# State-space layer of a hybrid backbone: its input projections put through the split 1 MB stream, inputs laid out beforehand, decay matrices merged

## Chip, cores, metric

One core of a Trainium2 chip. The metric is the device time of one launch in microseconds (us), over three runs.

## What is computed

Two layers work on 512 tokens of width 1024 (256 of context, 256 latent), in float32. Layer 0 is a state-space layer (SSD, 32 heads in 8 groups, state 128, chunks of 128 tokens, forward and backward) and a dense SwiGLU of width 2816. Layer 1 is windowed attention and eight SwiGLU experts of width 3584 (two for each token). Norms are scaled and shifted by rows computed from `silu(c) @ w_mod`. What the change touches is the state-space layer:

```python
zxbcdt = h @ w_in                       # 512 x 1024 by 1024 x 6208: z 2048, x 2048, B 1024, C 1024, dt 64
xbc = silu(depthwise_conv_same(xbc, conv_w, conv_b))          # 5 taps along the tokens
dt = softplus(dt_raw + dt_bias); a = -exp(a_log) * dt; acum = cumsum(a)       # in each chunk
decay = exp(where(lower, acum[i] - acum[j], -inf))
y = (C B^T * decay * dt) x + (C state) * exp(acum)            # and the same backward
out = gated_rmsnorm(y, z, norm_w) @ w_out                     # RMS in each of the 8 groups
```

## The kernel before

**Engines and order.** Each engine has one instruction stream in an order that is written out by hand. They meet at named semaphores (`gemm_done`, `tok_evac`, `st_op`, `y_ready` ...). SP issues nearly all DMAs in one such order too, so a wait in it holds back every later load. Tokens lie along the free axis (`hT` is 8 tiles of 128 features by 512 tokens).

**Start.** 22 small vectors are loaded as rows and transposed, x and ctx are loaded by tokens and transposed (32 transposes, L642), then four 2 MB pieces of `w_mod` give shift and scale of the first norm (L618, rows turned to columns at L628), and only then come the norm, the dt projection (L662) and the first projections (L673).

**The state-space loop.** `step(g)` runs for each of the 8 groups. TensorE: projections `gemm_tile` of group g+1 (six tiles: two of x, then B and C, two of z; 8 float32 matmuls of 128x128 by 512 each, which the profile counts as 16 instructions, L673), `group_norm(g-1)` (L699), `to_tokens(g)` (transposes and C B^T, L708 to L716), `states(g)` (L724), one piece of `w_mod` (`modulation`, L618), `outputs(g)` (L745), `turn_mod` (L628). VectorE: the convolution of group g+1 (L1686, L1688), gating (L1757, L1761), `segments` (acum_i - acum_j for 4 heads and both directions, L1699), the group's 1/RMS over 128x512 (L1659, L1664), `token_scales` (L1710, x times tail, x times dt), `decayed` (L1717, L1722), `state_ops` (L1730 to L1743), `skip` (L1750). ScalarE: evacuations (L1254, L1259, L1300), exponentials of the decays (L1303, L1306), silu (L1287), squares and root (L1313, L1296). GpSimd masks the segments (L577). SP fetches the rows of acum, spread over all partitions, with `load_rowb` (L425, two DMAs of 1 MB), once `y_ready` of the group before says that `rowb` is free.

**Behind the loop.** Weights come as 1 MB units through a ring of four (`d_raw`). For each, ScalarE rounds a high part (`dense_high`, L1219), VectorE subtracts it (`dense_low`, L1552), and TensorE adds three fp32r products for one float32 product (`thrice`, L793 to L795): `w_out`, the SwiGLU, qkv and `w_o`. The experts' 336 units are treated alike in a ring of 12 (L1435, L1950, L1052 to L1054).

## Time and profile before

| | |
|---|---|
| median of 3 runs (lowest, highest) | 2409.55 us (2407.49, 2412.07) |
| profiled execution, its own time | 2407.64 us |
| its span | 2405.7 us |
| busy: TensorE, VectorE, ScalarE, GpSimd | 93%, 64%, 47%, 2% |
| start until the first projection | 0 to 70.5 us |
| state-space loop, until group 7 is alone | to 550.9 us |
| end of group 7 and `w_out` | to about 695 us |
| SwiGLU, attention, router | to about 1350 us |
| experts | to the end |

The shares of busy time are means over stages with different limits. The chain of waits says which engine's work ended last in each stage; the lines say what one instruction costs.

### The profile page before, as it was taken

The page shows a single profiled execution, that of the slowest core. Times are in us where ns is not written, and L with a number is a line of the kernel's source. Part 1 is how long each engine was busy: PE and PEld are TensorE (multiplying, and loading weights), DVE is VectorE, ACT ScalarE, POOL GpSimd, SP SyncE. Part 2 cuts the span into 40 slices and gives each one's busy share as a digit, 9 for nine tenths or more (in the row PEclk, how much of TensorE's full clock was granted, in tenths as well). Part 3 has the DMA queues.
Part 4 walks back from the last instruction along what each step waited for, and adds up shares of the span by engine and source line. Part 5 has one row for each costly group of instructions (what it writes and reads, how often), then busy time and mean ns, then how long its engine had stood idle before and what let it go on. Part 6 is the DMA issues. An engine that isn't in the chain of part 4 may idle for free.

```text
span 2405.7 us, 27018 instructions
## 1 busy us (share of the span) xinstructions
PE 2238.5 (93%) x10771; PEld 1662.0 (69%) x10771; DVE 1539.7 (64%) x1554; ACT 1137.0 (47%) x1084; POOL 56.4 (2%) x21
## 2 busy tenths in 40 slices
PE   4999999996889999998898799999999999999997
PEld 3355555554767777786756688787878888887875
DVE  1387766666432333223585688887878788887885
ACT  1333333334232222224353676667666667676763
POOL 0030001111000000000000000000000000000000
PEclk8999999998989999998899899999999999999998
DMA  8243333321225545533600599999999989999990
GB/s 275 63 151 113 122 122 122 122 73 67 88 70 175 164 154 172 167 100 75 191 22 33 217 369 347 336 342 334 346 336 346 358 325 364 335 346 336 344 337 36
DMA packets 258467, 504.86 MB, mean 210 GB/s; under 512 B 34434, under 2 KB 148724, under 8 KB 256308
## 3 DMA queue, kind: packets, MB, share of 16 engines
q1 hardware_dynamic: 258276, 503.19, 59.8%
q8 instruction: 76, 1.25, 0.2%
q14 instruction: 35, 0.29, 0.0%
q10 hardware_dynamic: 80, 0.13, 0.0%
HBM read 502.08 MB, written 1.18 MB: 209 GB/s over the span
## 4 chain that ended last, share of the span: by engine, by line
PE 86%; DVE 3%; ACT 2%; issue 1%; DMA 0%; DVEq 0%; SPq 0%; ACTq 0%
PE ps L1054 13%; PE ps L1052 13%; PE ps L1053 13%; PE ps L673 11%; PE ps L793 8%; PE ps L795 7%; PE ps L794 7%; PE ps L745 3%; PE ps L963 1%; PE ps L981 1%; PE ps L1038 1%; PE ps L1111 1%; PE ps L1081 1%; PE ps L805 1%; PE ps L971 1%
## 5 line engine op out<-in xcount | busy, mean ns | idle before, releaser
L1950 DVE TENSOR_TENSOR w_lo<-w_raw,w_hi 128x2048 fp32r<-128x2048 f32 x336 | 749.4, 2286 | 52.1 <-ACT w_hi L1435 51.0
L1435 ACT ACTIVATE w_hi<-w_raw 128x2048 fp32r<-128x2048 f32 x336 | 626.6, 1920 | 79.5 <-PE ps L1054 79.0
L1052 PE MATMUL ps<-w_hi,x_hi 128*128 128x512 f32 x896 | 358.0, 400 | 2.0 <-DVE x_lo L2006 2.0
L1054 PE MATMUL ps<-w_hi,x_lo 128*128 128x512 f32 x896 | 355.5, 397 | 0.0
L1053 PE MATMUL ps<-w_lo,x_hi 128*128 128x512 f32 x896 | 352.3, 393 | 0.0
L673 PE MATMUL ps<-hT,ring 128*128 128x512 f32 x768 | 335.1, 594 | 2.5 <-ACT area L1279 2.5
L1552 DVE TENSOR_TENSOR d_lo<-d_raw,d_hi 128x2048 fp32r<-128x2048 f32 (+1 forms) x52 | 117.0, 2251 | 328.8 <-ACT d_hi L1219 328.8
L1219 ACT ACTIVATE d_hi<-d_raw 128x2048 fp32r<-128x2048 f32 (+1 forms) x52 | 97.8, 1881 | 374.3 <-DMA d_raw<-in_ffn_w 224.8
L673 PEld LDWEIGHTS ps<-hT,ring 128*128 128x128 f32 x768 | 144.1, 190 | 177.0 <-issue 174.2
L1054 PEld LDWEIGHTS ps<-w_hi,x_lo 128*128 128x128 f32 x896 | 168.2, 188 | 41.3
L1053 PEld LDWEIGHTS ps<-w_lo,x_hi 128*128 128x128 f32 x896 | 168.3, 188 | 40.1
L1052 PEld LDWEIGHTS ps<-w_hi,x_hi 128*128 128x128 f32 x896 | 168.3, 188 | 40.1 <-DVE x_lo L2006 2.2
L1052 PE MATMUL ps<-w_hi,h_hi 128*128 128x512 f32 x448 | 180.4, 403 | 1.4 <-DVE h_lo L2022 1.4
L793 PE MATMUL ps<-h_top,d_hi 128*128 128x512 f32 (+1 forms) x432 | 170.0, 394 | 9.9 <-DVE h_low L1544 9.9
L1054 PE MATMUL ps<-w_hi,h_lo 128*128 128x512 f32 x448 | 177.7, 397 | 0.0
L1053 PE MATMUL ps<-w_lo,h_hi 128*128 128x512 f32 x448 | 176.2, 393 | 0.0
L795 PE MATMUL ps<-h_top,d_lo 128*128 128x512 f32 (+1 forms) x432 | 166.0, 384 | 0.0
L794 PE MATMUL ps<-h_low,d_hi 128*128 128x512 f32 (+1 forms) x432 | 164.6, 381 | 0.0
L793 PEld LDWEIGHTS ps<-h_top,d_hi 128*128 128x128 f32 x432 | 82.8, 192 | 35.4 <-issue 18.0
L1054 PEld LDWEIGHTS ps<-w_hi,h_lo 128*128 128x128 f32 x448 | 84.1, 188 | 20.7
L1052 PEld LDWEIGHTS ps<-w_hi,h_hi 128*128 128x128 f32 x448 | 84.1, 188 | 20.6 <-DVE h_lo L2022 1.6
L1659 DVE RECIPROCAL area<-area 128x512 f32<-128x512 f32 x8 | 26.8, 3353 | 111.5 <-ACT area L1296 96.9
(275 smaller groups left out, 2969.0 us busy)
## 6 DMA issues: line engine op xcount, KB each, us to landing
w_raw<-in_moe_w SPq DMA_DIRECT2D x672, 512.0 KB, 4.5
d_raw<-in_ffn_w SPq DMA_DIRECT2D x60, 512.0 KB, 4.6
ring<-in_w_mod SPq DMA_DIRECT2D x48, 512.0 KB, 5.8
d_raw<-in_w_mod SPq DMA_DIRECT2D x48, 512.0 KB, 6.4
ring<-in_ssd_w_in SPq DMA_DIRECT2D x32, 512.0 KB, 5.1
area<-acum_rows SPq DMA_DIRECT2D x16, 1024.0 KB, 5.9
ring<-in_ssd_w_in SPq DMA_DIRECT2D x8, 1024.0 KB, 5.4
d_raw<-in_ssd_w_out SPq DMA_DIRECT2D x16, 512.0 KB, 4.9
```

The lines of the kernel that those rows point to most:

```text
L673: last = mm(ps[t % 2][:], wtile(slot, 8, 768, k, t * P), hT[:, k, :], start=k == 0, stop=k == KT - 1)
L745: last = mm(o, l, r, start=n == 0, stop=n == len(steps) - 1)
L793: mm(o, w[0], v[0], start=first, stop=False)
L794: mm(o, w[0], v[1], start=False, stop=False)
L795: return mm(o, w[1], v[0], start=False, stop=last)
L1052: mm(o, hi, w_hi[u % HIGH][:, a:a + 512], start=first, stop=False)
L1053: mm(o, hi, w_lo[u % RAW][:, a:a + 512], start=False, stop=False)
L1054: return mm(o, lo, w_hi[u % HIGH][:, a:a + 512], start=False, stop=last)
L1219: A(d_hi[si % D_HIGH][:, 0:w], d_raw[n % D_RAW][:, 0:w], ACT.Copy).then_inc(S["dhi_done"], 1)
L1435: A(w_hi[n % HIGH][:], w_raw[n % RAW][:], ACT.Copy).then_inc(S["whi_done"], 1)
L1552: TT(d_lo[n % D_RAW][:, 0:w], d_raw[n % D_RAW][:, 0:w], d_hi[si % D_HIGH][:, 0:w].bitcast(F32), ALU.subtract).then_inc(S["dlo_done"], 1)
L1950: TT(w_lo[n % RAW][:], w_raw[n % RAW][:], w_hi[n % HIGH][:].bitcast(F32), ALU.subtract)\
```

## The change

- `w_in` and layer 0's `w_mod` join the ring of 1 MB units. Each projection of a group is now three units ("x", "bc", "z") of 48 fp32r products, split by `dense_high` and `dense_low` as the later weights are. The norm's output is split too (`h_top`, `h_low_`), and so is the dt weight (`wdt`).
- All inputs are packed outside the kernel: x is stored transposed, the vectors as one 128x536 array, each unit of weights as 128 rows of 8 KB. The row loads, their transposes and those of x are gone. The experts' stream reads packed units as well.
- The first norm's shift and scale come in four pairs of units (`mod_pair`, `turn_pair`). After each pair two feature tiles of the norm are finished, and `gemm_part` takes these two of the first x projection.
- The mask is applied to `rowb` itself. `segments` is now on ScalarE: exp(acum_i + nb_j) with nb = ln(dt) - acum as bias, 32 ACTIVATEs of 128x128 in a group. Both directions are added (`merge`) and multiplied by C B^T once, and x times dt is gone. The outputs have 80 instead of 112 instructions. Only the 768 columns that carry a state are exponentiated and multiplied in `rowb` (`row_exps`, `carried`).
- The convolution's middle tap with its bias is on ScalarE (`tap`); the other four stay on VectorE, x and B/C apart.
- The group's RMS is summed into 128x128 and spread by TensorE (`group_sums`, `group_spread`).
- The gated rows of groups 2 to 5 are written to DRAM (`keep_group`) and read back into `hT`. The loops over groups are unrolled.

```diff
-    order = [("wout", j, h) for j, h in ((0, 0), (1, 0), (0, 1), (1, 1), (2, 0), (2, 1), (3, 0), (3, 1))]
+    order = [("m0", u, 0) for p in range(4) for u in (p, 4 + p)]
+    order += [("x", 0, 0), ("bc", 0, 0), ("z", 0, 0)]
+    for g in range(GROUPS):
+        if g + 1 < GROUPS:
+            order += [("x", g + 1, 0), ("bc", g + 1, 0)]
+        else:
+            order.append(("wout", 0, 0))
+        order += [("m0", 8 + 2 * g, 0), ("m0", 9 + 2 * g, 0)]
+        if g + 1 < GROUPS:
+            order.append(("z", g + 1, 0))
+    order += [("wout", j, h) for j, h in ((1, 0), (0, 1), (1, 1), (2, 0), (2, 1), (3, 0), (3, 1))]
...
+            def load_dense(n):
+                if D_BEFORE[n] is not None:
+                    sp.wait_ge(S["d_used"], D_BEFORE[n] + 1)
+                w = dense_width(DENSE[n]) // 2
+                for i in range(2):
+                    sp.dma_start(d_raw[D_SLOT[n]][:, i * w:i * w + w], dense[n, :, i * w:i * w + w])\
+                        .then_inc(d_in[D_SLOT[n]], 16)
...
             def load_rowb(g):
+                if g == 0:
+                    sp.wait_ge(S["scr_out"], 16)
+                else:
+                    sp.wait_ge(S["y_ready"], 2 * g)
...
+                    src = scr[d * HEADS + g * HPG:d * HEADS + g * HPG + HPG, :]
                     sp.dma_start(rowb[d], src.unsqueeze(0).to_broadcast([P, HPG, NTOK])).then_inc(S["rowb_in"], 16)
-            sp.dma_start(cst[:, 0:C_BAND], consts[:, 0:C_BAND]).then_inc(S["consts_in"], 16)
-            sp.dma_start(cst[:, C_IOTA:C_N], consts[:, C_IOTA:C_N]).then_inc(S["band_in"], 16)
-            sp.wait_ge(S["zero_done"], 1)
...
             for n, unit in enumerate(DENSE):
+                if n < 4 or unit == EARLY:
+                    continue
+                if unit[0] == "m0" and 8 <= unit[1] < 23 and unit[1] % 2:
+                    load_rowb((unit[1] - 9) // 2)
...
+            for g in range(GROUPS):
+                pl.wait_ge(S["rowb_in"], 32 * g + 32)
+                if g:
+                    pl.wait_ge(S["y_ready"], 2 * g)
                 for d in range(2):
-                    pl.wait_ge(S["seg_op"], 2 * g + d + 1)
-                    v = seg[d].rearrange("p h (c i) -> p (h c) i", c=NCH)
-                    pl.affine_select(out=v, in_=v, compare_op=ALU.is_ge, fill=-1e30, base=0,
+                    pl.affine_select(out=seg[d].rearrange("p h (c i) -> p (h c) i", c=NCH),
+                                     in_=rowb[d].rearrange("p h (c i) -> p (h c) i", c=NCH),
+                                     compare_op=ALU.is_ge, fill=-1e30, base=0,
                                      pattern=[[0, 16], [1 if d == 0 else -1, P]],
                                      channel_multiplier=-1 if d == 0 else 1).then_inc(S["seg_mask"], 1)
...
+            def gemm_part(kind, g, banks, ks):
+                n = D_AT[(kind, g, 0)]
+                dense_wait(n)
+                for k in ks:
+                    if g == 0:
+                        pe.wait_ge(S["n_low"], k + 1)
+                    for t in range(2):
+                        last = thrice(ps[banks[t]][:], dense_tile(n, k, t), (h_top[:, k, :], h_low_[:, k, :]),
+                                      k == 0, k == KT - 1)
+                return last
+            def group_sums(g):
+                pe.wait_ge(S["ysq_done"], 2 * g + 2)
+                pe.wait_ge(S["mod_done"], 5 + g)
                 for t in range(2):
-                    last = mm(ps[5][:], ones, ysq[:, t, :], start=t == 0, stop=t == 1)
+                    for c in range(NCH):
+                        last = mm(ps[4][32 * c:32 * c + 32, 0:P], ones[:, 0:32], ysq[:, t, c * P:c * P + P],
+                                  start=t == 0, stop=t == 1)
                 last.then_inc(S["gsum_done"], 1)
...
+                for c in range(NCH):
+                    pick = ident[:, 32 * c:32 * c + 1].to_broadcast([P, P])
+                    last = mm(ps[5][:, c * P:c * P + P], pick, grs, start=True, stop=True)
...
-                            steps = [(xdt[d][:, ch, c0:c0 + HD], seg[d][:, h, s]) for d in range(2)]
+                            steps = [(xtok[:, ch, c0:c0 + HD], seg[0][:, h, s])]
...
-            def step(i, first=False, more=True):
-                if more:
-                    gemm_tile(i + 1, 0, 0).then_inc(S["gemm_done"], 1)
-                    gemm_tile(i + 1, 0, 1).then_inc(S["gemm_done"], 1)
-                if not first:
...
-                if more:
-                    gemm_tile(i + 1, 0, 2).then_inc(S["gemm_done"], 1)
-                    gemm_tile(i + 1, 0, 3).then_inc(S["gemm_done"], 1)
-                states(i)
...
-                if more:
-                    gemm_tile(i + 1, 0, 4).then_inc(S["gemm_done"], 1)
-                    gemm_tile(i + 1, 0, 5).then_inc(S["gemm_done"], 1)
...
-            with pe.Fori(1, 7) as i:
-                step(i)
...
+            norm_sum(0)
+            for p in range(4):
+                mod_pair(p, 5 + p % 2)
+                turn_pair(p, 3 + p % 2)
+                if p == 0:
+                    norm_spread(0)
+                else:
+                    gemm_part("x", 0, (0, 1), (2 * p - 2, 2 * p - 1))
...
+            pe.wait_ge(S["mrow_sb"], 4)
+            for k in range(KT):
+                c = slice(P * k, P * k + P)
+                last = thrice(ps[6][:], (wdt_hi[:, c], wdt_lo[:, c]), (h_top[:, k, :], h_low_[:, k, :]), k == 0, k == KT - 1)
+            last.then_inc(S["dt_ps"], 1)
+            pe.wait_ge(S["gemm_evac"], 2)
+            gemm_part("bc", 0, (0, 1), range(KT)).then_inc(S["d_used"], 1)
+            pe.wait_ge(S["dt_dve"], 1)
...
+            pe.wait_ge(S["mod_done"], 4)
+            gemm_part("z", 0, (2, 3), range(4))
...
+            gemm_part("z", 0, (2, 3), range(4, KT)).then_inc(S["d_used"], 1)
...
+            for g in range(7):
+                if g:
+                    group_sums(g - 1)
+                pe.wait_ge(S["gemm_evac"], 6 * g + 4)
+                gemm_part("x", g + 1, (0, 1), range(4))
+                if g:
+                    group_spread(g - 1)
+                gemm_part("x", g + 1, (0, 1), range(4, KT)).then_inc(S["d_used"], 1)
+                to_tokens(g)
+                pe.wait_ge(S["gemm_evac"], 6 * g + 8)
+                gemm_part("bc", g + 1, (0, 1), range(4))
+                states(g)
+                gemm_part("bc", g + 1, (0, 1), range(4, KT)).then_inc(S["d_used"], 1)
+                pe.wait_ge(S["tok_evac"], 4 * g + 4)
+                mod_pair(4 + g, 5)
+                if g == 0:
+                    pe.wait_ge(S["ac_rows_sb"], 1)
+                outputs(g)
+                gemm_part("z", g + 1, (2, 3), range(KT)).then_inc(S["d_used"], 1)
+                turn_pair(4 + g, 4)
...
+            def tap(g, t):
+                act.wait_ge(S["gemm_evac"], 6 * g + t + 1)
+                if g:
+                    act.wait_ge(S["sk_done" if t < 2 else "ce_done"], 2 * g if t < 2 else 3 * g)
+                    act.wait_ge(S["tr_ready"], 4 * g)
+                A(cx[:, t, :].rearrange("p (s t) -> p s t", s=2), raw[:, t, :, 2:2 + 256], ACT.Identity,
+                  bias=vc(V_CB + conv_row(g, t)), scale=vc(V_CW + 64 + conv_row(g, t))).then_inc(S["tap_done"], 1)
...
+                if not g:
+                    act.wait_ge(S["nb_op"], 2)
+                for d in range(2):
+                    act.wait_ge(S["seg_mask"], 2 * g + d + 1)
+                    for h in range(HPG):
+                        for ch in range(NCH):
+                            v = seg[d][:, h, ch * P:ch * P + P]
+                            j = 32 * d + 4 * g + h
+                            last = A(v, v, ACT.Exp, bias=nb[:, ch, j:j + 1])
+                    last.then_inc(S["e_done"], 1)
...
+                act.wait_ge(S["e_done"], 2 * g + 2)
+                for d, c in CARRIED:
+                    v = rowb[d][:, :, c]
+                    A(v, v, ACT.Exp).then_inc(S["er_done"], 1)
...
+            for p in range(4):
+                one_tile(2 * p)
+                one_tile(2 * p + 1)
+                top_tile(0, 2 * p)
+                top_tile(0, 2 * p + 1)
+                if p == 0:
+                    dense_high(0)
+                if p == 1:
+                    act.wait_ge(S["wdt_in"], 16)
...
+                evac_z(g, 0)
+                evac_z(g, 1)
+                conv_silu(g, 2)
+                conv_silu(g, 3)
+                if g:
+                    group_root(g - 1)
+                dense_high(3 * g + 4)
+                segments(g)
+                evac_raw(g + 1, 0)
+                evac_raw(g + 1, 1)
+                token_evac(g)
+                row_exps(g)
+                dense_high(3 * g + 5)
+                tap(g + 1, 0)
+                tap(g + 1, 1)
+                evac_raw(g + 1, 2)
+                evac_raw(g + 1, 3)
+                if g < 6:
+                    dense_high(3 * g + 6)
+                tap(g + 1, 2)
+                tap(g + 1, 3)
+                conv_silu(g + 1, 0)
+                conv_silu(g + 1, 1)
+                y_squares(g)
...
+            def convolve(g, bc):
+                base = 16 * g + 8 * bc
+                for i, k in enumerate((0, 1, 3, 4)):
+                    for q in range(2):
+                        t = 2 * bc + q
+                        if i == 0:
+                            dv.wait_ge(S["tap_done"], 4 * g + t + 1)
+                        else:
+                            dv.wait_ge(S["conv_step"], base + 2 * (i - 1) + q + 1)
+                        dst = cx[:, t, :].rearrange("p (s t) -> p s t", s=2)
+                        STT(dst, raw[:, t, :, k:k + 256], vc(V_CW + 32 * k + conv_row(g, t)), dst, ALU.mult, ALU.add)\
+                            .then_inc(S["conv_step"], 1)
...
-            def segments(g):
-                dv.wait_ge(S["rowb_in"], 32 * g + 32)
+                return v[:, :, 32 * d + 4 * g:32 * d + 4 * g + 4]
+            def token_scales(g):
...
+            def merge(g):
+                dv.wait_ge(S["e_done"], 2 * g + 2)
+                TT(seg[0], seg[0], seg[1], ALU.add).then_inc(S["m_add"], 1)
+            def carried(g):
+                for i, (d, c) in enumerate(CARRIED):
+                    dv.wait_ge(S["er_done"], 3 * g + i + 1)
+                    v = rowb[d][:, :, c]
+                    TT(v, v, cx[:, 3, c].unsqueeze(1).to_broadcast([P, HPG, v.shape[2]]), ALU.mult)\
+                        .then_inc(S["ce_done"], 1)
...
+            for g in range(7):
+                if g:
+                    mod_out(3 + g)
+                    group_inverse(g - 1)
+                dense_low(3 * g + 4)
+                if g:
+                    finish(g - 1)
                 token_scales(g)
+                merge(g)
+                carried(g)
                 decayed(g)
                 state_ops(g)
                 skip(g)
-                convolve(g + 1)
-                mod_rows(4 + g, (5,), 512)
+                mod_rows(4 + g)
+                dense_low(3 * g + 5)
+                convolve(g + 1, 0)
                 gated(g)
-            dv.wait_ge(S["dcol_op"], 3)
-            convolve(0, first=True)
-            step(0, first=True)
-            with dv.Fori(1, 7) as g:
...
```

## Rows read from the trace of the kernel before

**Rows 1.** Windows: length, busy by engine, clock share, DMA share, GB/s.

```profile
40.00:60.00 20.00, 16.50 (x128) 10.49 (x128) 3.18 (x8) 0.37 (x1) 0.00 (x0) 0.59 1.07 328
...
1400.00:1500.00 100.00, 100.00 (x460) 81.63 (x459) 83.68 (x52) 69.59 (x49) 0.00 (x0) 1.00 0.97 355
```

**Rows 2.** Chain that ended last: start, length, what; outputs of groups 0, 3, 4, 6, 7, `w_out`'s end.

```profile
155.66 7.13 PE ps L745 x112
...
342.85 7.13 PE ps L745 x112
...
404.64 7.13 PE ps L745 x112
...
528.21 8.73 PE ps L745 x112
...
606.85 7.10 PE ps L745 x112
...
694.01 1.67 DVE xT L1809 x4
```

**Rows 3.** Waits of TensorE, 100 to 600 us: in total, times, longest.

```profile
PE ps L745 <- DVE ring L1743: 19.5, 7, 3.5
PE ps L699 <- DVE modT L1591: 15.5, 1, 15.5
```

**Rows 4.** The same chain in the SwiGLU: 48 fp32r matmuls lie between the rows.

```profile
722.03 1.00 PE ps L805 x16
734.33 0.34 PE ps L816 x4
734.67 1.00 PE ps L805 x16
```

**Rows 5.** Lines, 0 to 700 us: busy us, mean ns, idle before.

```profile
L1688 DVE SCALAR_TENSOR_TENSOR area<-area,col 128x512 f32<-128x512 f32 x128 | 85.5, 745 | 0.0
...
L1722 DVE TENSOR_TENSOR area<-area,ring 128x2048 f32<-128x2048 f32 x16 | 35.9, 2284 | 3.9 <-ACT area L1306 3.9
...
L1552 DVE TENSOR_TENSOR d_lo<-d_raw,d_hi 128x2048 fp32r<-128x2048 f32 x10 | 22.9, 2290 | 35.4 <-ACT d_hi L1219 35.4
...
L1219 ACT ACTIVATE d_hi<-d_raw 128x2048 fp32r<-128x2048 f32 x10 | 19.1, 1909 | 38.3 <-PE ps L795 27.7 <-PE ps L618 6.4 <-DMA d_raw<-in_ssd_w_out 4.2
...
L724 PE MATMUL ps<-area 128*128 128x256 f32 x96 | 22.0, 379 | 0.0
```

**Rows 6.** TensorE in order of time: start, length.

```profile
30.39 3.64 PE L618 MATMUL ps<-ring,csT 128*32 128x512 f32 x32 [1.31 <-issue]
...
70.47 14.00 PE L673 MATMUL ps<-hT,ring 128*128 128x512 f32 x32
85.19 0.71 PE L684 MATMUL ps<-cst,area 64*128 64x64 f32 x8 [0.72 <-DVE area L1644]
...
114.28 0.60 PE L694 MATMUL ps<-cst,acum 128*64 128x128 f32 x4
```

**Rows 7.** GpSimd's masks (source view): ns, least, median, most.

```profile
L577 POOL TENSOR_SCALAR_AFFINE_SELECT area<-area x16: 1997/2163/12979, 132.2 to 568.8; 128x2048 f32<-128x2048 f32 x16
```

**Rows 8.** ScalarE's short operations in order of time: start, length together.

```profile
30.70 4.26 ACT L1171 ACTIVATE area<-xT 128x512 f32<-128x512 f32 x8 [16.20 <-DMA rw<-in_moe_router]
...
60.61 7.97 ACT L1189 ACTIVATE hT<-hT,modT,alpha 128x256 f32<-128x256 f32 x16 [3.94 <-DVE hT L1534]
...
100.75 0.45 ACT L1271 ACTIVATE acum<-ps 128x128 f32<-128x128 f32 x2 [0.28 <-PE ps L690]
101.21 1.28 ACT L1273 ACT_TABLE_LOAD   x1
```

**Rows 9.** Waits, 1340 us to the end: TensorE's longest in the experts.

```profile
PE ps L1081 <- DVE xT L2028: 6.1, 7, 0.9
```

**Rows 10.** DMA issues: number, KB each, median us to landing.

```profile
w_raw<-in_moe_w SPq DMA_DIRECT2D x672, 512.0 KB, 4.5
...
area<-acum_rows SPq DMA_DIRECT2D x16, 1024.0 KB, 5.9
```

More of the change, by code:

```diff
@@ L105, with dense_places, dense_width @@
 D_HIGH = 2
-def dense_arrivals():
-    total, out = [0] * D_RAW, []
-    for n, x in enumerate(DENSE):
-        total[n % D_RAW] += 64 if x[0] in ("q", "wo") else 32
-        out.append(total[n % D_RAW])
-    return out
-D_ARRIVED = dense_arrivals()
-W2_K = ((0, 8), (8, 8), (16, 6))
+W0 = 3 * GROUPS
+W2_K = ((0, 8), (8, 8), (16, 6))
+EARLY = ("x", 0, 0)
+MOD_PAIRS = [(p, 4 + p) for p in range(4)] + [(2 * p, 2 * p + 1) for p in range(4, 12)]
+def dense_places():
+    slot, before, arrived = [], [], []
+    last, total, ring = [None] * (D_RAW + 1), [0] * (D_RAW + 1), 0
+    for n, unit in enumerate(DENSE):
+        u = D_RAW
+        if unit != EARLY:
+            u = ring % D_RAW
+            ring += 1
+        total[u] += 32
+        slot.append(u)
+        before.append(last[u])
+        arrived.append(total[u])
+        last[u] = n
+    return slot, before, arrived
+D_SLOT, D_BEFORE, D_ARRIVED = dense_places()
+def dense_width(unit):
+    return 256 * (W2_K[unit[2]][1] if unit[0] == "w2" else KT)
 STREAM = expert_stream()
@@ new lines, in _ @@
+            last = mm(ps[4][:, 256:512], ones, atk, start=True, stop=True)
+            last.then_inc(S["ac_ps"], 1)
+            gemm_part("z", 0, (2, 3), range(4, KT)).then_inc(S["d_used"], 1)
+            pe.wait_ge(S["ac_sb"], 1)
+            for ch in range(NCH):
+                last = pe.transpose(ps[6][0:64, ch * P:ch * P + P], acum[:, ch, :], ident)
+            last.then_inc(S["ac_rows"], 1)
+            for g in range(7):
[13 more added lines that the diff above has]
+                mod_pair(4 + g, 5)
+                if g == 0:
+                    pe.wait_ge(S["ac_rows_sb"], 1)
+                outputs(g)
+                gemm_part("z", g + 1, (2, 3), range(KT)).then_inc(S["d_used"], 1)
+                turn_pair(4 + g, 4)
@@ L1322, in _ @@
+            evac_z(7, 0)
+            evac_z(7, 1)
+            conv_silu(7, 2)
+            conv_silu(7, 3)
+            group_root(6)
+            dense_high(W0)
             gate_high(0)
-            dense_high(0)
+            segments(7)
+            token_evac(7)
             gate_high(1)
-            act.wait_ge(S["gsum_done"], 7)
-            A(grs, ps[5][:], ACT.Sqrt, bias=eps, scale=1.0 / 256).then_inc(S["grs_done"], 1)
-            for n in range(4):
-                act.wait_ge(S["tr_ready"], 28 + n + 1)
-                dst = (xtok[:, 0:2, :], xtok[:, 2:4, :], btok, cbT)[n]
-                A(dst, ps[2 + n][:], ACT.Copy).then_inc(S["tok_evac"], 1)
@@ L1342, in _ @@
-            for t in range(2):
-                act.wait_ge(S["yg_done"], 14 + t + 1)
-                A(ysq[:, t, :], yb[:, t, :], ACT.Square).then_inc(S["ysq_done"], 1)
-            dense_high(3)
-            act.wait_ge(S["gsum_done"], 8)
-            A(grs, ps[5][:], ACT.Sqrt, bias=eps, scale=1.0 / 256).then_inc(S["grs_done"], 1)
+            dense_high(W0 + 2)
+            y_squares(7)
+            dense_high(W0 + 3)
+            group_root(7)
             gate_high(4)
             gate_high(5)
-            dense_high(4)
@@ L1761, in gated @@
                     TT(yb[:, t, :], yb[:, t, :], zs[:, t, :], ALU.mult).then_inc(S["yg_done"], 1)
-            def step(g, first=False):
-                segments(g)
-                if not first:
-                    mod_out(0, 12 + 4 * g, 4, 3 + g, 5)
-                    finish(g)
+            dense_low(2)
+            dv.wait_ge(S["dcol_op"], 3)
+            convolve(0, 0)
+            dv.wait_ge(S["ac_ps"], 1)
+            TS(nb, dtk, 1e-37, None, ALU.max).then_inc(S["nb_op"], 1)
+            convolve(0, 1)
+            dv.wait_ge(S["nb_ln"], 1)
+            dv.wait_ge(S["ac_sb"], 1)
+            TT(nb, nb, acum, ALU.subtract).then_inc(S["nb_op"], 1)
+            dv.wait_ge(S["ac_exp"], 1)
+            TT(tail, ps[4][:, 256:512].rearrange("p (c h) -> p c h", c=NCH), acum, ALU.subtract).then_inc(S["ac_tail"], 1)
+            dense_low(3)
+            dv.wait_ge(S["ac_exp"], 2)
+            TT(tail, tail, dtk, ALU.mult).then_inc(S["ac_tail"], 1)
+            dv.wait_ge(S["ac_tail"], 2)
+            for g in range(7):
+                if g:
+                    mod_out(3 + g)
+                    group_inverse(g - 1)
+                dense_low(3 * g + 4)
+                if g:
+                    finish(g - 1)
                 token_scales(g)
+                merge(g)
+                carried(g)
                 decayed(g)
```

1020 lines of the change are left out of this document (458 added, 562 removed).

## The prediction

> **What bounds the kernel now.** I read the page first: its shares of busy time (the table above) put TensorE far ahead. A mean over stages does not price a change in one of them, so the windows came next. Between 1400 and 1500 us TensorE is busy all the time at the full granted clock while DMA moves 355 GB/s [rows 1], and TensorE's longest wait in the experts is 6.1 us in seven pieces, none of it on a load [rows 9]. There the packed layout is worth nothing unless it slows the stream. The change lives in the first 700 us, and there I read the chain that ended last: outputs of group 0 end at 162.79 us, of group 6 at 536.94, of group 7 at 613.95, and `w_out` ends at about 694.0 [rows 2]. In the loop one group takes 404.64 - 342.85 = 61.79 us; the six periods take 374.15, or 62.4 each. Only then the waits: of a group's 61.8 us TensorE waits only 19.5/7 = 2.8 us for the state operations [rows 3]. So the loop is TensorE's own work, and the reader should see that only less work, or the same work faster, moves it.
>
> **TensorE's work in a group.** 96 instructions of float32 projection take 3 x 14.0 = 42 us, because 32 take 14.00 [rows 6]. After it 48 fp32r matmuls stand for 32 such instructions. In the SwiGLU 48 of them, 4 short ones (0.34 us) and 16 for a piece of `w_mod` (1.00 us) fill 734.67 - 722.03 = 12.64 us [rows 4]: (12.64 - 1.34)/48 = 0.235 us each, 11.2 us a unit, 33.7 us a group. Bounds: 0.217, the mean of all 460 in the window of the experts [rows 1], and 0.43 at half clock. That is 8.3 us less. The outputs lose 32 of 112 instructions, which take 7.13 us [rows 2]: 5.1, so 2.0 less. The rest stays within 0.5 us (root sums 0.5 and spread 1.0 for 1.9; two 1 us units of `w_mod` for 1.9). From 61.8 less the wait of 2.8, TensorE's work falls by 10.8 to about 48 us.
>
> **The other two engines.** VectorE gains three `dense_low` (3 x 2.29, [rows 5]) and one addition of 128x2048 (2.24, as L1722's 35.9/16). It loses the segments (eight two-input operations of 128x512; priced like L1688's 85.5/128 = 0.67 they are 5.3), x times dt (two of 128x1024, 2.2), one of two 2048-wide products by C B^T (2.24), a quarter of the two by C (1.1) and four first taps, and the reciprocal becomes a quarter as wide. 9.1 come and at least 10.8 go: no more work than now. ScalarE gains three `dense_high` (3 x 1.91), four taps (0.7 each) and the 32 exponentials of 128x128. No row shows these with a bias. Two copies of 128x128 take 0.45 together, so 0.22 each; eight of 128x512 take 4.26, 0.53 each; sixteen of 128x256 with bias and scale per partition take 7.97, 0.50 each, where the line through the first two would give 0.33 [rows 8]. One operand per partition is then worth half of 0.17: 0.31 each, 9.9 us a group. Bounds 0.22 and 0.50. It loses two exponentials of 128x2048 and a quarter of two more, some 5 us, so it gains 13 to 14. Neither engine comes to TensorE's 48, so what decides is who waits for whom.
>
> **One period by hand.** Time 0 is the end of outputs(g). TensorE: z to 11.2, `turn_pair` to 12.0. VectorE, which began `skip` when the outputs began at -5.1, does `mod_rows`, `dense_low` of z and the x taps (8 x 0.67) until 4.0, gating to 6.5, `dense_low` of x to 8.8, the B/C taps to 14.1. `mod_out` stands behind them, and `group_sums` waits for it: a new wait of TensorE, 12.0 to 14.4, with all projections queued behind. Half of x to 20.4, spread to 21.4, other half to 26.9, `to_tokens` to 29.2. ScalarE: silus to 15.4, table load 1.28 [rows 8], root 17.1, `dense_high` 19.0, table load 20.3, exponentials to 30.2, evacuation of x to 31.3. TensorE's first half of B/C needs those banks: second new wait, 29.2 to 31.4. Then 36.9, states (22.0/8 = 2.75 [rows 5]) 39.6, second half 45.1, `w_mod` 47.1. ScalarE's token copies end at 33.4, row exponentials at 36.2. VectorE: scales 34.8, merge 37.0, `carried` (3072 columns, 3.4) 40.4, product 42.6, state operations 46.8 (4.2; they end 4.8 after the states now, the wait of 2.8 and a `w_mod` piece of 2). Outputs 47.1 to 52.2. VectorE and TensorE arrive together. Some five handovers between engines lie on this path; 0.1 us for each rounds it to 52.5 us. Six periods: 6 x (62.4 - 52.5) = **59 us**.
>
> SP waits for `y_ready` before `load_rowb`, with the next `w_mod` unit and z queued behind it. Neither is needed for 20 us, and 7 MB in 52 us is 140 GB/s against 355 reached [rows 1]: hidden. The rows take some 8 us from the end of the outputs (5.9 to landing [rows 10], issue and waits). Spill and reload of the gated rows go by queue and lie beside this. With four slots each unit is requested at least two units ahead; without that cover a unit costs its 4.5 to 6 us each time.
>
> **The mask.** Of the 16 masks the shortest takes 2.00 us, the median 2.16, one 12.98 [rows 7]. That one began in group 0 when VectorE worked without a gap on pairs of inputs in SBUF, and it ended 2 us after VectorE stopped. So it has to find VectorE idle. By my schedule the rows land at 8, VectorE is idle from 14.3 until the root's reciprocal at 17.1, and two masks end by 18.5, before the exponentials want them at 20.3. That is a margin of 1.8 us. The Trainium skill (SBUF — State Buffer, Who interferes with whom) says that VectorE operations with two SBUF inputs and GpSimd operations that read SBUF exclude each other for a whole instruction, whichever starts first. By that rule, the trace agrees (12.98 against 2.16), and a mask that slips between two taps would hold the taps up by 2 us as well.
>
> **Start and group 0.** Before, the first projection starts at 70.47. After, 4.5 MB precede the first pair of `w_mod` units (15.5 us at 328 to 355 GB/s with some 2 us to begin). A pair takes 3.64 at the clock there (32 instructions [rows 6]), then copy, turn, `mod_out`, alpha, two tiles on ScalarE, their tops and lows. TensorE alternates pair and quarter of x; I get x finished at 64 instead of 84.5, with quarters at half clock (12 x 0.43), dt at 70, B/C at 81. The dt chain on VectorE and ScalarE is unchanged (85.19 - 70.47 = 14.7 us, from the dt matmuls' end to the transposes that wait for it), so z waits until 86.5 and ends at 98.6; acum is turned at 99.2 instead of 114.3 to 114.9. From there the rows must go to DRAM and come back (an estimate of 14 us: copies and issues, 5 out, 5.9 back [rows 10]), two masks, then the exponentials with nothing beside them: x of group 1 is evacuated only at 126, and TensorE waits some 15 us. Outputs end at 148.8 instead of 162.8: **14 us**. Bounds: 25, if the quarters run at full clock and loads come as asked; 0, if pair, copy, turn and tile follow one another with 2 us more in each of four rounds and the dt chain stretches.
>
> **Group 7 and w_out.** Before, TensorE waits 15.5 us in front of `group_norm` (first unit of `w_out` asked only then, segments behind it on VectorE) [rows 3]. After, the unit is there, but `gate_high(1)` stands behind segments and token copies on ScalarE, so the second half of `out_part(0, 0)` waits some 10 us. By the same bookkeeping outputs(7) ends 71.3 after outputs(6) instead of 77.0: **5.7 us**. Then 694.0 - 613.95 = 80 us become 73, since the splits for `out_part(0, 1)` are done during outputs(7) and the root is short: **7 us**. Behind that nothing changes.
>
> **Sum.** 59 + 14 + 5.7 + 7 = 85.7 us off the profiled execution's own 2407.64 (span 2405.7, 1.94 around it): 2321.9. The median of the runs shown is 1.9 above that execution: **2324**.
>
> **Rivals.**
> - *The mask misses its gap* (0.17). The next idle time of VectorE comes after `finish` at 22.8; the exponentials start at 24.9, 4.6 later, and all behind them. Seven times 4.6 is 32: 2356. For: the margin of 1.8 us. Against: the segments no longer fill VectorE.
> - *The short exponentials cost far more* (0.13). At 0.41, midway to the bound, 32 x 0.10 = 3.2 us in each of seven groups: 2346; at the bound of 0.50, 2367.
> - *TensorE closes its two waits* (0.13), because the B/C taps end early and the exponentials cost 0.22: 48.5 us a group, 24 less: 2300.
> - *The first projection is not begun earlier in effect* (0.03): group 0 ends as now, 2338.
> - *Slower than before: the packed experts' stream* (0.03). A unit's 4 KB pieces are now 8 KB apart, where the `w2` units were one run. 672 loads of 512 KB are 352 MB [rows 10]; 1024 us at 344 GB/s. At the 328 GB/s of the first weights [rows 1] they take 1074: 2374. Below 317 GB/s they take over 86 us more, and the change loses. Against: no wait for a load there now. The Trainium skill (DMA: Bandwidth & Descriptors, Latency and other measured facts) warns of row pitches at large powers of two, measured from 512 KiB on. No run here shows one.
> - The forecast itself: 0.51, own range 2309 to 2341.
>
> **Numbers.** The cases above from 2300 to 2356 hold over 0.9; unknown prices and a start between 0 and 25 us widen each by 10. I give 2292 to 2362. Within 0.2% (4.8 us) is what the measurement cannot tell from no change. Faster 0.95, same 0.02, slower 0.03.
>
> **What would show it.** Outputs of neighbouring groups 52 to 53 us apart; two waits of TensorE in each period, on `modT` and on the evacuation of x, 2 us each; masks of 2 us that end before the exponentials; the short exponentials near 0.31 us each; group 0's outputs ending near 149; the experts' stage as long as now. A period over 57 us, masks over 5 us, or a wait on a unit's load would make the prediction wrong.

## The result, and the profile after

The changed kernel takes 2299.35 us (median of 4 runs, 2299.00 to 2299.93). The kernel before took 2410.81 beside it (2407.49 to 2412.93). The ratio is 0.9539, interval 0.9523 to 0.9556: 4.6% faster. The forecast was 2324 with a range of 2292 to 2362; the gain is 25 us larger than forecast. The profiled execution took 2299.07 us (span 2297.3). Against its span the gain is 22.7 us larger (108.4 against 85.7, table below); the other 2 us were added in the forecast for the median of the runs.

The outputs are again the marks. In order of time on TensorE (start, length), groups 0, 2, 6 and 7:

```profile
134.61 4.86 PE L766 MATMUL ps<-area 128*64 128x128 f32 x80
...
235.16 4.86 PE L766 MATMUL ps<-area 128*64 128x128 f32 x80
...
436.87 4.86 PE L766 MATMUL ps<-area 128*64 128x128 f32 x80
...
510.05 4.86 PE L766 MATMUL ps<-area 128*64 128x128 f32 x80
```

Their ends against those of [rows 2]:

| stage | before, us | after, us | gain | forecast |
|---|---|---|---|---|
| start and group 0 | 162.79 | 139.47 | 23.3 | 14 |
| six periods | 374.15 (62.4 each) | 302.26 (50.4 each) | 71.9 | 59 |
| group 7 | 77.0 | 73.2 | 3.8 | 5.7 |
| `w_out`, to 588.28 | 80.0 | 73.4 | 6.7 | 7 |
| the rest | 1711.7 | 1709.0 | 2.7 | 0 |
| sum | 2405.7 | 2297.3 | 108.4 | 85.7 |

The waits of TensorE from 100 to 600 us (total, times, longest) answer to [rows 3]:

```profile
PE ps L704 <- DVE modT L1655: 9.2, 7, 1.5
PE ps L647 <- ACT area L1248: 8.3, 3, 7.0
PE ps L647 <- DVE g_lo L1621: 7.6, 2, 5.2
...
PE ps L631 <- DVE cst L1644: 3.6, 1, 3.6
PE ps L713 <- DVE area L1748: 3.1, 1, 3.1
```

The first line is the new wait on `mod_out` (1.47 us in every period; a short one follows in group 7). The second, on the evacuation of x, is 7.0 us once, in group 0, and 0.7 or less in the loop, where 2.2 were forecast each time. One period in order of time on TensorE (189.43 to 240.02; the projections lie between the rows):

```profile
200.60 0.95 PE L631 MATMUL ps<-cst 128*128 128x2 f32 x8
203.02 0.65 PE L704 MATMUL ps<-area,cst 128*32 128x128 f32 x16 [1.47 <-DVE modT L1655]
...
210.82 1.05 PE L713 MATMUL ps<-area,cst 128*128 128x128 f32 x8
...
225.06 2.75 PE L744 MATMUL ps<-area 128*128 128x256 f32 x12
...
233.30 1.93 PE L622 MATMUL ps<-d_raw,csT 128*32 128x256 f32 x32
```

The 24 products behind this wait, half of the projection of x, take 7.38 us between 203.60 and 210.98; the same 24 take 5.84 in the period from 290.64, from 304.81 on. The windows (length, busy by engine, clock share, DMA share, GB/s) say why:

```profile
204.00:211.00 7.00, 7.00 (x26) 5.58 (x25) 3.25 (x2) 6.96 (x14) 2.63 (x2) 0.76 0.17 68
305.00:311.00 6.00, 6.00 (x29) 4.93 (x29) 3.25 (x2) 5.96 (x10) 2.84 (x2) 1.00 0.24 93
```

So four of the six periods are 50.5 to 50.6 us long (a wait of 1.47 and 1.5 us lost to the clock behind it) and two are 49.96 (the same wait, full clock, then 0.65 on the evacuation). TensorE's own work is 50.59 - 1.47 - 1.54 = 47.6; 48 was forecast. ScalarE in the same period, in order of time:

```profile
204.78 0.37 ACT L1275 ACTIVATE area<-ps,small 128x128 f32<-128x128 f32 x1
...
208.26 9.48 ACT L1287 ACTIVATE area<-area,atk 128x128 f32<-128x128 f32 x32
217.65 1.05 ACT L1248 ACTIVATE area<-ps 128x512 f32<-128x512 f32 x2
```

The exponentials begin 18.8 us into the period (forecast 20.3) and take 0.296 each (0.31). GpSimd's masks and VectorE's B/C taps there, and the masks of all groups in the source view (ns: least, median, most), to be read beside [rows 7]:

```profile
200.29 6.34 POOL L587 TENSOR_SCALAR_AFFINE_SELECT area<-area 128x2048 f32<-128x2048 f32 x2 [43.62 <-DMA area<-acum_rows]
```

```profile
197.42 5.38 DVE L1742 SCALAR_TENSOR_TENSOR area<-area,col 128x512 f32<-128x512 f32 x8
```

```profile
L587 POOL TENSOR_SCALAR_AFFINE_SELECT area<-area x16: 2001/2008/4768, 102.3 to 454.9; 128x2048 f32<-128x2048 f32 x16
```

The rows arrive while the taps still run (to 202.72): the masks begin 10.9 us into the period, where the rows were forecast to land at 8. The first mask ends 2 us after the taps, the pair at 206.63, before the exponentials.

### The profile page after: what moved, and what is told of

It is laid out like the page before. It is cut to its first block, busy times and chain, and to the rows that moved or that the text cites. A ratio compares the mean times of both kernels' runs of the same rounds, so it can differ in the third digit from the quotient of the medians.

```text
span 2297.3 us, 27395 instructions
## 1 busy us (share of the span) xinstructions
PE 2161.5 (94%) x11224; PEld 1729.8 (75%) x11224; DVE 1495.1 (65%) x1479; ACT 1236.9 (54%) x1394; POOL 45.7 (2%) x20
## 3 DMA queue, kind: packets, MB, share of 16 engines
q8 instruction: 90, 1.47, 0.3%
## 4 chain that ended last, share of the span: by engine, by line
PE 83%; DVE 7%; ACT 4%; issue 1%; DVEq 0%; ACTq 0%
PE ps L1048 14%; PE ps L1046 14%; PE ps L1047 13%; PE ps L647 10%; PE ps L649 10%; PE ps L648 10%; DVE area L1742 3%; DVE d_lo L1613 2%; PE ps L957 1%; PE ps L975 1%; PE ps L1032 1%; PE ps L1105 1%; ACT area L1287 1%; PE ps L1075 1%; PE ps L659 1%
## 5 line engine op out<-in xcount | busy, mean ns | idle before, releaser
L1613 DVE TENSOR_TENSOR d_lo<-d_raw,d_hi 128x2048 fp32r<-128x2048 f32 (+1 forms) x76 | 171.9, 2262 | 334.4 <-ACT d_hi L1219 334.4
L647 PE MATMUL ps<-h_top,d_hi 128*128 128x512 f32 (+1 forms) x816 | 331.5, 406 | 25.2 <-DVE h_low L1605 9.8
L1219 ACT ACTIVATE d_hi<-d_raw 128x2048 fp32r<-128x2048 f32 (+1 forms) x76 | 143.7, 1890 | 382.8 <-DMA d_raw<-in_dense 245.2
L649 PE MATMUL ps<-h_top,d_lo 128*128 128x512 f32 (+1 forms) x816 | 322.9, 396 | 0.0
L648 PE MATMUL ps<-h_low,d_hi 128*128 128x512 f32 (+1 forms) x816 | 319.1, 391 | 0.0
L647 PEld LDWEIGHTS ps<-h_top,d_hi 128*128 128x128 f32 x816 | 158.3, 194 | 69.6 <-issue 26.2
L649 PEld LDWEIGHTS ps<-h_top,d_lo 128*128 128x128 f32 x816 | 158.1, 194 | 35.7
L648 PEld LDWEIGHTS ps<-h_low,d_hi 128*128 128x128 f32 x816 | 158.9, 195 | 33.6
L1047 PEld LDWEIGHTS ps<-w_lo,h_hi 128*128 128x128 f32 x448 | 84.2, 188 | 19.9
```

Source lines behind the costliest of these rows:

```text
L647: mm(o, w[0], v[0], start=first, stop=False)
L648: mm(o, w[0], v[1], start=False, stop=False)
L649: return mm(o, w[1], v[0], start=False, stop=last)
L1047: mm(o, hi, w_lo[u % RAW][:, a:a + 512], start=False, stop=False)
L1219: A(d_hi[si % D_HIGH][:, 0:w], d_raw[u][:, 0:w], ACT.Copy).then_inc(S["dhi_done"], 1)
L1613: TT(d_lo[u][:, 0:w], d_raw[u][:, 0:w], d_hi[si % D_HIGH][:, 0:w].bitcast(F32), ALU.subtract)\
```

## The experiments

A period below is the distance between the ends of neighbouring outputs. Kernels that ran on one chip are compared with each other; the others by their ratio to the kernel before and by their rows.

**1. Float32 on the high parts.** In `gemm_part` of the changed kernel:

```
-  last = thrice(ps[banks[t]][:], dense_tile(n, k, t), (h_top[:, k, :], h_low_[:, k, :]), ...)
+  last = mm(ps[banks[t]][:], dense_tile(n, k, t)[0].bitcast(F32), h_top[:, k, :].bitcast(F32), ...)
```

> The 48 triples of fp32r products of a group's projections become 48 float32 matmuls on the high parts alone (the low parts are still made, and left out of the sum). Sixteen float32 matmuls of this shape took 14.00 us in the kernel before, 0.875 each; a triple takes 3 x 0.235 = 0.70. Theory A (TensorE's own work sets the period): 48 x 0.17 = 8.3 us more per group, period 50.6 to about 58.5, whole kernel +50 to +60 us (2350 to 2360). Rival B (the gain came from the shorter waits and the work taken off the sides, and TensorE has room): under +15 us.

2338.23 us, ratio 0.9692 (0.9673 to 0.9712): 39 us more, short of the 50. The period is 55.7, the 16 matmuls of z take 14.00 us where the 48 products take 11.42, and what remains of the wait is 0.35:

```profile
312.20 14.00 PE L694 MATMUL ps<-h_top,d_hi 128*128 128x512 f32 x32
326.04 0.95 PE L631 MATMUL ps<-cst 128*128 128x2 f32 x8
327.33 0.64 PE L704 MATMUL ps<-area,cst 128*32 128x128 f32 x16 [0.35 <-DVE modT L1655]
```

A period's projections take 42.2 us instead of 34.8, 7.4 more, but the period grows by 5.3: the slower TensorE loses no clock and hardly waits. TensorE's work bounds this kernel, and the faster products gave away 2 of their 7.4 us.

**2. One product of three.**

```
-  last = thrice(ps[banks[t]][:], dense_tile(n, k, t), (h_top[:, k, :], h_low_[:, k, :]), ...)
+  last = mm(ps[banks[t]][:], dense_tile(n, k, t)[0], h_top[:, k, :], ...)
```

> Only the product of the two high parts is left in a group's projections; the two products with a low part are left out. TensorE's work falls by 96 x 0.235 = 22.6 us a group. Theory A (TensorE and the chain exponentials, evacuation, scales, merge, carried, product, state operations, outputs are nearly tied; VectorE was 1.5 us ahead at the outputs): the period falls by a few us only, to 45 to 48, whole kernel -15 to -40 us. Rival B (TensorE alone sets the period, the others have ample room): the period falls to about 30, whole kernel near -150 us.

2297.77 us, ratio 0.9524 (0.9503 to 0.9544): no gain at all, less than either theory expected. TensorE's waits from 139 to 440 us:

```profile
PE ps L704 <- DVE modT L1655: 58.5, 6, 11.5
PE ps L694 <- ACT area L1248: 35.3, 6, 6.5
PE ps L766 <- DVE area L1811: 26.8, 6, 5.0
```

20 us a period are handed back as waits. The periods are 48.5 and 48.7 (two of the six) or 52.8 to 54.3 (four). In the long ones the masks begin 0.4 to 1.2 us after the first tap and hold the others up (GpSimd, then VectorE):

```profile
194.31 4.58 POOL L587 TENSOR_SCALAR_AFFINE_SELECT area<-area 128x2048 f32<-128x2048 f32 x2 [47.90 <-DMA area<-acum_rows]
```

```profile
193.87 8.87 DVE L1742 SCALAR_TENSOR_TENSOR area<-area,col 128x512 f32<-128x512 f32 x8
```

The eight taps take 8.87 us instead of 5.38. The outputs run at a lower granted clock here (6.2 to 7.6 us long), so their ends blur the periods. The x taps of neighbouring groups on VectorE give the length of the other chain, the one over VectorE and ScalarE:

```profile
290.25 5.38 DVE L1742 SCALAR_TENSOR_TENSOR area<-area,col 128x512 f32<-128x512 f32 x8
...
339.91 5.38 DVE L1742 SCALAR_TENSOR_TENSOR area<-area,col 128x512 f32<-128x512 f32 x8
```

It is 49.66 us long where no mask stops the taps, and 53.15 where one does (237.10 to 290.25). That is 2 us more than TensorE's own 47.6 and 0.7 less than the changed kernel's mean period of 50.4: the two chains are nearly tied. The unchanged total hides two things: the six periods together grew by 9.6 us (to 311.9), by the stopped taps, and groups 0 and 7 became 5.6 and 4.6 us shorter (133.9 and 68.6).

**3. Wide exponentials.**

```
-  for h in range(HPG):
-      for ch in range(NCH): ... last = A(v, v, ACT.Exp, bias=nb[:, ch, j:j + 1])
+  last = A(seg[d], seg[d], ACT.Exp)
```

> The 32 exponentials of 128x128 with a bias become two of 128x2048 without one (leaves out -acum_j and the factor dt in the decays). ScalarE: 9.5 us become about 3.7 in each group. Theory A (in the loop TensorE's work binds and the exponentials have a margin of about 1.5 us): next to nothing in the six periods (0 to -1 us each), the gain in group 0 and group 7, where TensorE waits for the evacuation (7.0 us) and for g_lo (5.2 us): -8 to -14 us in all. Rival B (the short exponentials are on the path in every group): 8 x 5.8 = -46 us.

2282.77 us, ratio 0.9464 (0.9446 to 0.9483), 16.6 less, a little over theory A. Group 0 ends 7.2 us earlier (132.31) and group 7 takes 65.6 instead of 73.2. The six periods together take 300.45 instead of 302.26. The price of a short exponential, which had a rival of its own, counts in two groups of eight (14.8 of the 16.6 us).

**4. The first projection behind all pairs.**

```
-  else:
-      gemm_part("x", 0, (0, 1), (2 * p - 2, 2 * p - 1))
-  gemm_part("x", 0, (0, 1), (6, 7)).then_inc(...)
+  gemm_part("x", 0, (0, 1), range(KT)).then_inc(...)
```

> The first projection of x is issued whole after the four w_mod pairs, in place of one quarter behind each pair. Theory A (the quarters fill TensorE's waits between pairs): x ends later, by the three quarters of 3.1 to 5.3 us that no longer lie in the waits, less what full clock gives back: +4 to +9 us. Rival B (pairs wait for their loads and quarters only delay the next pair's chain): 0 or a gain of up to 3 us.

2300.22 us (2297.89 to 2303.28), ratio 0.9533 (0.9513 to 0.9554): by time no difference that these runs resolve. By the trace, that of the slowest of the four runs, outputs(0) end at 143.97 instead of 139.47 and the span is 2301.5. So the quarters between the pairs are worth about 4.5 of the 23.3 us by these two traces. Experiments 5, 6 and 7 leave the start as it was and end outputs(0) at 139.71, 140.95 and 141.65, so the 4.5 is uncertain by some 2 us.

**5. Masks twice.** In GpSimd's loop, a first `affine_select` with the same operands counts on a semaphore that the second waits for.

> Each mask is made twice, the second time over the first's output place, and the exponentials wait for the second. In the changed kernel a pair of masks ran from 200.29 to 206.6 us and the exponentials started at 208.26. Theory A (the prediction's step: a margin of 1.8 us, measured 1.7, stands against the pair): the exponentials start 2.4 us or more later in each group, +2.4 to +5 us a period, +15 to +35 us in all. Rival B (the exponentials of a direction wait for the mask of that direction alone, so the first needs only half of the pair and the second has another 4.7 us): the masks end in time, 0 to +3 us in all, unless they meet VectorE's operations after 207 us and hold these up.

2299.64 us, ratio 0.9538 (0.9519 to 0.9557): nothing, rival B. The four masks of one group (GpSimd), and the exponentials (ScalarE):

```profile
200.61 4.32 POOL L587 TENSOR_SCALAR_AFFINE_SELECT area<-area 128x2048 f32<-128x2048 f32 x1 [37.55 <-DMA area<-acum_rows]
205.06 2.01 POOL L593 TENSOR_SCALAR_AFFINE_SELECT area<-area 128x2048 f32<-128x2048 f32 x1
207.02 2.00 POOL L587 TENSOR_SCALAR_AFFINE_SELECT area<-area 128x2048 f32<-128x2048 f32 x1
209.17 3.86 POOL L593 TENSOR_SCALAR_AFFINE_SELECT area<-area 128x2048 f32<-128x2048 f32 x1
```

```profile
208.52 9.49 ACT L1293 ACTIVATE area<-area,atk 128x128 f32<-128x128 f32 x32
```

The last mask ends at 213.03, just when the second half of the exponentials begins. It collides with `dense_low`, which takes 3.93 instead of 2.29 us, where VectorE had been idle before its next wait.

**6. Experts from the original layout.** `load_unit` of the kernel before, with `mw1`, `mw3` and `mw2` as inputs.

> The experts' weights are read from their original layout, as in the kernel before, in place of the packed one. TensorE never waited for a load there in either kernel, though a load took 4.5 us to land before and 5.7 after. Theory A (hidden both ways): 0, within 3 us. Rival B (the packed pieces with their pitch of 8 KB cost the stream something): 5 to 20 us less than the changed kernel.

2299.85 us, ratio 0.9536 (0.9516 to 0.9556): nothing. The page's DMA issues (KB each, median us to landing) of this kernel, then of the changed one:

```profile
w_raw<-in_moe_w SPq DMA_DIRECT2D x672, 512.0 KB, 4.6
```

```profile
w_raw<-in_experts SPq DMA_DIRECT2D x672, 512.0 KB, 5.7
...
area<-acum_rows SPq DMA_DIRECT2D x16, 1024.0 KB, 8.4
```

The packed pieces land 1.1 us later, and TensorE waits for no load in either; between 1400 and 1500 us both read 334 to 336 GB/s.

**7 and 8. Taking away the wait on `mod_out`, and unloading VectorE.** Kernel 7: `turn_pair(p)` for p from 4 on writes PSUM bank 5 in place of 4, `mod_out` reads it there, and in `group_sums`

```
-  pe.wait_ge(S["mod_done"], 5 + g)
```

Kernel 8 keeps this and adds on ScalarE, behind `dense_high(3 * g + 5)`, what VectorE loses:

```
+  A(stt_[:, 0, :], ps[2][:, 0:256], ACT.Copy)
+  A(stt_[:, 3, :], ps[3][:, 256:512], ACT.Copy)
+  A(yb[:, t, :], cx[:, t, :], ACT.Copy, scale=dcol[...])       # skip
...
+  A(mrow[:, a:a + 512], ps[5][:], ACT.Copy)                    # mod_rows, behind the x taps
```

> The turned piece of w_mod goes to bank 5 in place of bank 4, so that group_sums need not wait for mod_out. Measured so far: the wait is 1.47 us in each period, and in half of the periods the eight k-tiles behind it take 7.4 instead of 5.8 us at a lower granted clock. Theory A (TensorE's wait and its clock set the period; the vector-scalar chain has room, 48.5 us in the shortest periods of the run with one product): period 50.3 to about 48.3, -10 to -15 us in all. Rival B (the chain over VectorE and ScalarE is as long as TensorE's work and its wait, and only moves the wait elsewhere): TensorE waits for the evacuation of x or the state operations instead, 0 to -4 us.

> As the kernel with bank 5, and skip, the copy of the w_mod rows and the two state copies go from VectorE to ScalarE, 2.4 us a group off the chain that VectorE carries from the end of the exponentials to the B/C taps. If the chain over VectorE and ScalarE is the tied limit (rival B above), the period falls here to TensorE's own 47.9 us: -15 to -20 us against the changed kernel. If TensorE alone was the limit (theory A above), this is no faster than the kernel with bank 5 by more than 3 us.

On one chip: 2306.7 us (ratio 0.9564, 0.9545 to 0.9584) and 2289.74 (0.9497, 0.9477 to 0.9516). Kernel 7 is 7 us slower than the changed kernel by the medians. The ratios' intervals just overlap, but experiments 5 and 6, as fast as the changed kernel, ran on the same chip and never took more than 2300.95 us, while kernel 7 never took less than 2305.79. Five of its periods are 51.5 and one is 49.95, 51.3 on average instead of 50.4; neither theory had that. Its waits from 139 to 440 us, the place in one period, and the windows behind the wait:

```profile
PE ps L647 <- ACT area L1247: 13.2, 6, 2.2
```

```profile
219.23 1.06 PE L735 MATMUL ps<-area 128*128 128x128 f32 x8
222.49 0.51 PE L647 MATMUL ps<-h_top,d_hi 128*128 128x512 f32 x1 [2.21 <-ACT area L1247]
```

```profile
222.50:229.90 7.40, 7.40 (x25) 5.91 (x26) 6.46 (x5) 6.52 (x8) 0.00 (x0) 0.77 0.02 7
```

The 1.47 us before the root sums have become 2.21 before B/C, and the lost clock now lies behind the evacuation of x, that is in the loop exponentials, evacuation, B/C, `w_mod` piece, its rows on VectorE (idle 1.7 us for them), taps, silu, root, exponentials. That loop is 51.5 us long in five of six periods; in the sixth the clock is full behind the same wait. Kernel 8 shortens VectorE's part: 49.4 in every period, with a wait of 1.66 for the evacuation. That is 17 us less than kernel 7, so the chain over VectorE and ScalarE was a limit, but only 9.6 less than the changed kernel, where 15 to 20 were expected: the wait for the evacuation stayed.

**9 to 11. The evacuation earlier, and the tail.**

```
 for ch in range(NCH):
+    if g < 7 and (d, h, ch) == (1, 2, 0):
+        evac_raw(g + 1, 0)
+        evac_raw(g + 1, 1)
...
 segments(g)
-evac_raw(g + 1, 0)
-evac_raw(g + 1, 1)
```

Kernel 9 is kernel 7 with this edit, kernel 10 is kernel 8 with it, and kernel 11 adds the new order in group 7.

> As the kernel with bank 5, and the two evacuations of x stand after 24 of the 32 exponentials in place of behind all of them; x ends after about 21 of them there, and nothing else on ScalarE comes later by it. In the run with bank 5 TensorE waited 2.2 us for them in each period, the next 24 products took 7.4 in place of 5.8 us, and the chain through w_mod's rows, VectorE's taps and the exponentials followed. Theory A (that wait and its clock made the kernel with bank 5 slower): period 51.5 to about 49.8, where VectorE and ScalarE alone would be: -9 to -13 us against it, near 2295. Rival B (the exponentials themselves close the loop, wherever the evacuation stands): no change, 2305 to 2308.

> As the kernel with the small operations on ScalarE, with the same move of the evacuation. There TensorE waited 1.66 us for it in each period of 49.5. Theory A: the wait goes, the period comes to TensorE's own work of 47.9 to 48.3 us, -8 to -11 us against it (near 2280). Rival B (TensorE then waits for the state operations by as much): 0 to -3 us.

> As the run before, and in group 7 gate_high(1) stands between the exponentials of the two directions, gate_low(1) before token_scales, the split of the second w_out unit before decayed, and turn_pair(11) behind out_part(1, 0). In the changed kernel TensorE waits 5.2 us for g_lo, 3.6 for the w_mod rows and 3.1 for the root's inverse between outputs(6) and outputs(7). Expected: the first two of these waits go and a new one of about 4 us for the state operations stands before out_part(1, 0): -4 to -8 us against the run before.

On one chip: 2299.9 us (0.9545, 0.9529 to 0.9561), 2280.16 (0.9467, 0.9451 to 0.9482) and 2276.0 (0.9451, 0.9435 to 0.9466). TensorE's waits from 139 to 440 us in kernel 9, then in kernel 10:

```profile
PE ps L712 <- DVE area L1748: 6.9, 3, 2.3
PE ps L765 <- DVE area L1811: 6.4, 5, 1.3
PE ps L647 <- ACT area L1247: 3.3, 4, 1.3
```

```profile
PE ps L765 <- DVE area L1837: 1.7, 6, 0.3
```

Kernel 9 is 6.8 us faster than kernel 7, where 9 to 13 were expected. It has three periods of 49.2 to 49.7, as theory A said, and three of 53.2: there the masks begin about 1 us after the first B/C tap (0.8 in one: 250.12 and 249.32) and the taps take 8.87 us, as in experiment 2. Kernel 10, 9.6 us faster than kernel 8, has 47.85 in all six: TensorE's own work and a wait of 0.3. Kernel 11 is 4 us faster still: two waits of group 7 (5.2 and 3.6 in the changed kernel, 6.3 and 2.1 in kernel 10) go, and one of 6.8 for the state operations comes where about 4 were expected. It is the fastest of all, 1% below the changed kernel; the two intervals do not touch.

## Why the prediction was right, and where it was off

- **What bounds the kernel.** Right: TensorE's work fell by what the rows gave (48 forecast, 47.6 to 47.85 measured), and slower products cost time (experiment 1). That the two chains "arrive together" was in the hand-made period, and experiment 2 shows how nearly: with 23 us less work for TensorE the other chain still takes 49.66 us where nothing stops it.
- **The period, 52.5 against 50.4.** The mis-sized term is the two waits. I had 2.4 + 2.2 us and five handovers; measured are 1.47 on `mod_out` in each, then either 1.5 of lost clock or 0.65 on the evacuation. The B/C taps ended at 13.3 instead of 14.1, so the exponentials began 1.5 us earlier. Six times 2.1 is 13 of the 25 us. The lost clock, 1.5 us in four periods, was no term of mine at all. Experiments 3 to 6 show it too, in three or four periods of six.
- **Faster products.** Forecast 8.3 us a period, 7.4 in the trace of experiment 1, 5.3 in the period. All other gains of the period (12.0 less 5.3) come from less work on TensorE and the wait of 2.8 us that went; no run separates merged decays from short root sums and the units of `w_mod`.
- **Start and group 0, 14 against 23.3.** The rivals had it "not earlier in effect"; it was earlier by more. x was finished at 53.9 (64 forecast), B/C at 70.95 (81), acum turned at 91.4 (99.2), outputs at 139.47 (148.8). The step that failed is the price of a pair of `w_mod`, 3.64 us, and of a quarter of x, 5.2 us (12 x 0.43). The row of 3.64 [rows 6] was misread: its 32 instructions have 512 columns, those of a pair 256, and the granted clock over it was full. The kernel before, over that row and over the next piece of `w_mod` (length, busy by engine, clock share, DMA share, GB/s):

```profile
30.40:34.00 3.60, 3.60 (x33) 1.13 (x33) 0.69 (x1) 3.30 (x7) 0.00 (x0) 1.00 0.18 18
...
40.40:44.00 3.60, 3.60 (x17) 0.62 (x17) 0.00 (x0) 0.00 (x0) 0.00 (x0) 0.50 1.05 387
```

  The next piece, as large as a pair, took 3.64 at a share of 0.50. So both prices were those of half clock. In the changed kernel the first two pairs took 4.5 and 4.0 us, with 0.6 of wait for the second unit in each, and the first quarter 5.3 at a clock share of 0.52. The third and fourth pair ran at full clock, 1.93 each, and the other three quarters took 3.0 each. Two pairs 1.7 us shorter and three quarters 2.1 shorter are 9.8 us by price alone, about the 10 by which x came earlier:

```profile
36.89 1.93 PE L622 MATMUL ps<-d_raw,csT 128*32 128x256 f32 x32
...
43.52 1.93 PE L622 MATMUL ps<-d_raw,csT 128*32 128x256 f32 x32
```

```profile
40.00:60.00 20.00, 18.18 (x109) 13.87 (x109) 8.10 (x14) 9.13 (x15) 0.00 (x0) 1.00 0.60 201
```

  Behind that the way from acum to the evacuation of x took 24.7 us (91.4 to 116.1) where 26.8 were forecast, for the masks began after 10.9 us and not 14; TensorE's wait for it was 7.0 and not 15. The bound of 25, "if the quarters run at full clock", was the better estimate. The quarters' place between the pairs is worth about 4.5 (experiment 4); packed inputs, fewer transposes and cheaper pairs share the rest, which no run took apart.
- **The mask.** The mechanism was right, the margin was misread. I set 1.8 us between the pair's end and the first exponential (measured 1.6), but a direction's exponentials wait for its own mask alone, so the second has 4.7 us more. Doubling every mask cost nothing (experiment 5). A mask that slips among the taps holds them up, as forecast, but by more than the 2 us I gave it: a pair made the eight taps 3.5 us longer in experiments 2 and 9. The Trainium skill (SBUF — State Buffer, Who interferes with whom) lets a VectorE operation with two SBUF inputs and a GpSimd operation that reads SBUF block each other for a whole instruction, whichever is issued first; the traces agree, with 8.87 against 5.38 us. The forecast of this was right and its side wrong: the danger is an early mask, not a late one. That the changed kernel misses it is luck: the rows took 8.4 us to land and not 5.9. Landing at 8 us, as forecast, they would have met the first tap, by these rows (197.42 is 8.0 into the period).
- **Short exponentials.** 0.296 against 0.31, and outside groups 0 and 7 their price hardly shows (1.8 us in six periods, experiment 3).
- **TensorE closes its waits** (2300) named the right time for a wrong reason: the waits did not close, the periods stayed 1.9 us above its 48.5, and the start gave 9 us more.
- **Group 7 and `w_out`.** 3.8 against 5.7 and 6.7 against 7: the wait on `gate_high(1)` was 5.2 us and not 10, and 3.6 on the `w_mod` rows and 3.1 on the root's inverse, which I had not listed, took more than that back.
- **The experts' stream.** Hidden either way (experiment 6). The rest of the program became 2.7 us shorter; no cause was looked for.

## What to carry to other kernels

When two chains of a loop are nearly equally long, speeding up one engine gains only until the other chain binds, and taking away one wait can cost time: here it moved the wait to a place inside the loop, and five of six periods became 51.5 us long. Unload the second chain as well, and put the operation that the wait is for where it is due; together these edits gave 19 us, and the loop then ran at TensorE's own work. Before you take a duration from a row, look at the number and shape of its instructions and at the granted clock of its own window, and before you set a margin, look at which semaphore value each consumer waits for.

## What the runs showed of the hardware

- A wait of 1.47 us of TensorE, behind 0.95 us of eight matmuls with two columns each, is followed in four periods of six by 24 products at a granted share of 0.77 to 0.81, 1.5 us longer than at 1.00; in the other two by full clock. A wait of 2.2 was followed by 0.77 in five periods and by 1.00 in the sixth (kernel 7), one of 1.66 by 1.00 in all six (kernel 8). What decides it stays open.
- With one product of three TensorE was busy 63% of the time from 200 to 400 us, and the granted share there was 0.73 to 0.83; the outputs then took 6.2 to 7.6 us instead of 4.86. Less work on TensorE made its other work slower.
- Masks on GpSimd that meet VectorE's run of eight taps either wait for its end (one mask then takes up to 5.6 us instead of 2.0) or stop it (5.38 to 8.87 us). In experiments 2 and 9, masks that began 0.4 to 1.2 us after the first tap stopped the run (seven cases), and those that began 1.6 to 4.3 us after it waited (seven cases); in the changed kernel they begin 2.9 us after it (200.29 and 197.42) and wait.
